# Moving the sampled keys, the softmax sums and the value rounds to earlier steps of a hybrid decoder layer

## The reference, cut to what matters

```
k_all = concatenate([ck[page_table], k]);  v_all = concatenate([cv[page_table], v])
s = einsum('bqhd,bkhd->bhqk', q, k_all) * dh ** -0.5 + c[past] - c[keys]
p = softmax(s, axis=-1)
out = einsum('bhqk,bkhd->bqhd', p, v_all)
```

## Time and profile before

| what | value |
|---|---|
| median of 3 runs | 1890.67 us (1890.24 to 1895.3) |
| the profiled execution's own time | 1893.1 us |
| its span, first to last instruction | 1891.4 us |
| PE busy, share of the span | 1803.2 us, 95% |
| DVE busy | 730.6 us, 39% |
| mean granted TensorE clock | 0.962 of full speed |
| pairs 0 to 3, from the first tile's scores of each | 102.33, 192.09, 282.94 and 372.26 us to 463.55 us |
| value rounds 0 to 15 | 450.68 to 553.74 us |

### The profile page before, as it was taken

The page is one execution under the profiler, slowest core; times in us unless marked ns, Lnnn a source line. Parts: engine busy times, 40 slices in busy tenths (PEclk is TensorE's granted clock), DMA queues, the critical chain, the costliest instruction groups (busy, mean ns, idle before and its releaser), DMA issues.

```text
span 1891.4 us, 29215 instructions
## 1 busy us (share of the span) xinstructions
PE 1803.2 (95%) x11360; PEld 1632.1 (86%) x11360; DVE 730.6 (39%) x1303; ACT 363.3 (19%) x691; POOL 502.5 (27%) x295
## 2 busy tenths in 40 slices
PE   5999999998999999999999989999999999999994
PEld 5966666665777879999999979999999999999993
DVE  3156766542415443121138754223213313312318
ACT  3132222322413223111120340100000010010022
POOL 3310101100210303332234524223232233322225
PEclk8999999998987979999999989999999999999997
DMA  5134434302642201111112212111111111111102
GB/s 155 54 108 122 118 116 117 122 25 80 180 143 47 56 8 50 44 44 54 46 34 72 63 34 59 54 44 44 44 44 53 36 55 44 44 46 54 45 23 90
DMA packets 173120, 126.39 MB, mean 67 GB/s; under 512 B 22266, under 2 KB 146570, under 8 KB 173042
## 3 DMA queue, kind: packets, MB, share of 16 engines
q1 hardware_dynamic: 169490, 124.09, 22.3%
q10 hardware_dynamic: 3552, 1.25, 0.3%
HBM read 115.45 MB, written 9.85 MB: 66 GB/s over the span
## 4 chain that ended last, share of the span: by engine, by line
PE 88%; DVE 5%; issue 2%; DMA 2%; ACT 2%; POOL 1%; SPq 1%; POOLq 0%; ACTq 0%; DVEq 0%
PE psum L741 14%; PE psum L745 14%; PE psum L744 14%; PE psum L819 4%; PE psum L825 4%; PE psum L823 4%; PE psum L1277 4%; PE psum L1276 4%; PE psum L1272 4%; PE psum L974 4%; PE psum L947 2%; PE psum L1225 2%; PE psum L1229 2%; PE psum L1228 2%; PE psum L950 1%
## 5 line engine op out<-in xcount | busy, mean ns | idle before, releaser
L689 POOL CAST wh<-raw 128x1024 fp32r<-128x1024 f32 x132 | 143.5, 1087 | 1342.9 <-PE psum L819 436.4
L741 PE MATMUL psum<-xh,wh 128*128 128x344 f32 (+1 forms) x1488 | 478.6, 322 | 6.5 <-POOL wl L691 3.6
L745 PE MATMUL psum<-xh,wl 128*128 128x344 f32 (+1 forms) x1488 | 476.4, 320 | 0.0
L744 PE MATMUL psum<-xl,wh 128*128 128x344 f32 (+1 forms) x1488 | 476.2, 320 | 0.0
L691 POOL TENSOR_TENSOR wl<-raw,wh 128x1024 fp32r<-128x1024 f32 x132 | 328.8, 2491 | 10.6
L741 PEld LDWEIGHTS psum<-xh,wh 128*128 128x128 f32 x1488 | 280.8, 189 | 7.6 <-issue 7.3
L744 PEld LDWEIGHTS psum<-xl,wh 128*128 128x128 f32 x1488 | 280.8, 189 | 0.2
L745 PEld LDWEIGHTS psum<-xh,wl 128*128 128x128 f32 x1488 | 280.7, 189 | 0.0
L2320 DVE TENSOR_TENSOR hf<-sg,psum 128x344 f32<-128x344 f32 x66 | 33.8, 513 | 385.0 <-PE psum L745 385.0
L819 PE MATMUL psum<-xh,wh 128*128 128x352 f32 (+1 forms) x480 | 164.0, 342 | 1.1 <-DVE negc_tok L1840 1.1
L823 PE MATMUL psum<-xl,wh 128*128 128x352 f32 (+1 forms) x480 | 161.2, 336 | 0.0
(11 more groups left out here) (305 smaller groups left out, 2621.8 us busy)
## 6 DMA issues: line engine op xcount, KB each, us to landing
raw<-in_w_in SPq DMA_DIRECT2D x86, 256.0 KB, 3.3
parts<-in_cache_k SPq DMA_DIRECT2D x64, 256.0 KB, 3.0
parts<-in_cache_v SPq DMA_DIRECT2D x64, 256.0 KB, 2.9
raw<-in_w_gate SPq DMA_DIRECT2D x44, 256.0 KB, 3.1
raw<-in_w_up SPq DMA_DIRECT2D x44, 256.0 KB, 3.2
raw<-in_w_down SPq DMA_DIRECT2D x44, 256.0 KB, 2.7
raw<-in_w_o SPq DMA_DIRECT2D x28, 256.0 KB, 3.0
cb<-negc_scratch SPq DMA_DIRECT2D x8, 520.0 KB, 5.3
```

The lines of the kernel that those rows point to most:

```text
L689: pool.tensor_copy(wh[:, s, :], raw[:, r, :]).then_inc(sem("panel_high"), 1)
L741: first = mm(out, w[0], x[0], start=(n == 0), stop=False)
L744: mm(out, w[0], x[1], start=False, stop=False)
L745: last = mm(out, w[1], x[0], start=False, stop=(n == len(ks) - 1))
```

## The change

Three lists of step numbers and one new list are edited, and the calls in the programs of PE, DVE, ACT and SP follow them. The keys' parts stood in 32 of the steps 3 to 51 (pairs 0, 1 and 2: 10, 12 and 10 parts); they now stand in every step from 3 to 34 (15 parts in pair 0, 17 in pair 1). The sums move closer together by one step and the exponentials from step 12 to 11. Value rounds 0 to 5 stand in steps 12 to 17 of pair 3, with the first two samples' outputs in steps 15 and 17; ten rounds are left for the front in place of twelve, each sample's outputs now ahead of the next sample's first round, and the last output ahead of the turned values. The panel loads in SP's program move with the rounds.

```diff
-KEYS_AT = [3 + 50 * c // PARTS for c in range(PARTS)]
-SUMS_AT = {8: (1, 2), 10: (3,), 11: (4,), 13: (5,)}
-ROUNDS_AT = {14: 0, 15: 1, 16: 2, 17: 3}
+KEYS_AT = [3 + c for c in range(PARTS)]
+SUMS_AT = {8: (1, 2), 9: (3,), 10: (4,), 12: (5,)}
+ROUNDS_AT = {12 + r: r for r in range(6)}
+OUTPUTS_AT = {15: 0, 17: 1}
...
-            for r in range(4, ROUNDS):
-                p = {4: 21, 6: 22, 9: 23, 12: 24}.get(r)
+            for r in range(6, ROUNDS):
+                p = {6: 21, 8: 22, 11: 23, 14: 24}.get(r)
...
+                    if x in OUTPUTS_AT:
+                        sample_outputs(OUTPUTS_AT[x])
                     if x in ROUNDS_AT:
                         value_round(ROUNDS_AT[x])
                 for _ in range(HALF_SLICE):
                     next(filler, None)
-            sample_outputs(0)
...
             whole(G0 - 1, 1, "gate")
-            value_round(4)
-            sample_outputs(1)
+            sample_outputs(2)
+            value_round(6)
             whole(G0 - 1, 2, "gate")
-            value_round(5)
+            value_round(7)
             whole(G0, 0, "q")
-            value_round(6)
-            sample_outputs(2)
+            sample_outputs(3)
+            value_round(8)
...
             whole(G0 + 2, 1, "v0")
-            value_round(13)
+            value_round(15)
             whole(G0 + 2, 2, "v0")
-            value_round(14)
-            sample_outputs(6)
...
             turn((ke,), FRONT["kt"], [])
-            value_round(15)
+            sample_outputs(7)
...
             whole(G0 + 3, 0, "v1")
-            sample_outputs(7)
...
-                if (j, x) == (3, 12):
+                if (j, x) == (3, 11):
                     act.wait_ge(sem("sdiff_ready"), 2)
...
-                    if x == 16:
-                        own(0)
-            own_out(0)
-            own(1)
+                    if x in (14, 16):
+                        own((x - 14) // 2)
+                    if x in (15, 17):
+                        own_out((x - 15) // 2)
+            own(2)
```

More of the change, by code:

```diff
@@ L1078, in _ @@
             whole(G0 - 1, 1, "gate")
-            value_round(4)
-            sample_outputs(1)
+            sample_outputs(2)
+            value_round(6)
             whole(G0 - 1, 2, "gate")
-            value_round(5)
+            value_round(7)
             whole(G0, 0, "q")
-            value_round(6)
-            sample_outputs(2)
+            sample_outputs(3)
+            value_round(8)
             whole(G0, 1, "q")
-            value_round(7)
+            value_round(9)
             whole(G0, 2, "q")
-            value_round(8)
-            sample_outputs(3)
+            sample_outputs(4)
+            value_round(10)
             whole(G0 + 1, 0, "k")
-            value_round(9)
+            value_round(11)
             whole(G0 + 1, 1, "k")
-            value_round(10)
-            sample_outputs(4)
+            sample_outputs(5)
+            value_round(12)
             whole(G0 + 1, 2, "k")
-            value_round(11)
+            value_round(13)
             whole(G0 + 2, 0, "v0")
-            value_round(12)
-            sample_outputs(5)
+            sample_outputs(6)
+            value_round(14)
             whole(G0 + 2, 1, "v0")
-            value_round(13)
+            value_round(15)
             whole(G0 + 2, 2, "v0")
-            value_round(14)
-            sample_outputs(6)
             for b in FRONT["k"]:
@@ L2079, in _ @@
             logits(0, FRONT["logits"])
-            own_out(1)
-            own(2)
+            own_out(2)
+            own(3)
             decay_rows(0)
             decayed_q(0, FRONT["q"][0])
-            own_out(2)
+            own_out(3)
             decayed_q(1, FRONT["q"][1])
-            own(3)
+            own(4)
             decayed_q(2, FRONT["q"][2])
-            own_out(3)
+            own_out(4)
             decayed_k(0, FRONT["k"][0])
-            own(4)
+            own(5)
             decayed_k(1, FRONT["k"][1])
-            own_out(4)
+            own_out(5)
             decayed_k(2, FRONT["k"][2])
-            own(5)
-            own_out(5)
             own(6)
```

## The result

The changed kernel takes 1896.6 us in the median (1888.9 to 1903.7, 20 runs); the kernel before took 1893.0 us (1888.1 to 1897.4, 20 runs) beside it. The ratio is 1.0021, 95% interval 1.0012 to 1.0031: slower, by 2 to 6 us. Twenty runs of each resolve less than the 0.3% that the prediction took for the limit. The profiled execution took 1895.1 us with a span of 1893.4, 2.0 us more than before.

The account below looks back on a forecast made before the run. PE's own work was taken to bound the pairs, the value rounds' transfers the pace after them. Waits +6.5 and clock +2.0 from denser keys, -5.2 from sums and rounds, made +3.3 us: 1894.0 us, range 1886 to 1904.

Parts of the forecast that it names:

- part 2: Moved sums and value rounds, pair 3 and the front: -5.2 us in all, between -3.1 and -6.9.
- step 11 of pair 1: PE waits 3.1 us for the k2 unit, behind DVE's query wait, key part and division.
- step 16 of pair 0: PE waits longer for DVE's last copy, behind a late query and the part of step 15: +2.1 us.
- step 5 of pair 1: Key parts of steps 3 and 4 hold up maxima, repeating pair 0's 0.94 us wait: +1.0 us.
- step 6 of pair 0: A small added wait of PE from the denser keys: some 0.3 us.
- clock, part 1: Clock falls after PE's waits in the pairs with denser keys: +2.0 us, two falls of 1.39 less one.
- part 1: Denser keys in pairs 0 and 1: +6.5 us of PE waits, with 2.0 us more for the clock.
- waits, part 2: From pair 3 on: output inside a wait -1.05, moved rounds +0.2, front -0.4, round 15 -1.9; together -3.1 us.
- clock, part 2: Half-speed instructions regain speed: an output -0.8, round 15 -0.9, the turn after it about -0.4 us.
- (A): SP becomes the bound in pairs 0 and 1, all seven query changes reach PE: +13, 1904 us; chance 0.30 with (C).
- (B): DVE's waits stay within PE's slack except step 5 of pair 1: gain 4 to 6 us, 1885 to 1887; chance 0.25.
- (C): Rounds keep their transfers' pace and gain only the 1.99 us: whole +6.5, 1897 us; chance 0.30 with (A).

Follow-up runs that it names:

- Experiment 6: Changed kernel with no key part in step 9 of pair 1, its eight later parts one step on; 1892.57 us, ratio 1.0011 to the kernel before.
- experiment 3: Changed kernel with two query buffers, each sample's query loaded one sample ahead; 1889.89 us, ratio 0.998 to the kernel before.
- experiment 9: Changed kernel with value rounds 14 and 15 each one chunk later; 1897.99 us, ratio 1.0029 to the kernel before.
- Experiment 10: Changed kernel with the last rounds, 14 and 15, exactly in the order of the kernel before; 1901.16 us, ratio 1.0041 to the kernel before.
- experiment 2: Changed kernel with the keys' parts back in their old steps, so only the rounds' change remains; 1886.9 us, ratio 0.9964 to the kernel before.
- experiment 4: Changed kernel with the 64 small forget-value loads moved on SP from pairs 0 and 1 to pair 2; 1892.7 us, ratio 0.9994 to the kernel before.
- experiment 7: Changed kernel with two query buffers and no key part in steps 4 and 9 of any pair; 1884.59 us, ratio 0.9964 to the kernel before.
- 8: Changed kernel with two query buffers and the keys' parts in their old steps; 1885.37 us, ratio 0.9965 to the kernel before.
- 1: Kernel before with only the keys' 32 parts moved to steps 3 to 34; 1902.87 us, ratio 1.0048 to the kernel before.
- 5: Changed kernel with only round 15 put back behind the turned keys, last output behind a chunk; 1894.3 us, ratio 1.0014 to the kernel before.

## Why the prediction came out as it did

The sign and the size of the whole were right: +3.3 us predicted, +2.0 in the profiled spans and +3.6 in the medians. The median itself lies 2.6 us above the 1894.0, nearly all of it because the kernel before also ran 2.3 us slower in these runs than in those that the prediction was set against. That part 2 came out near its -5.2 us is luck, as two errors in it cancel (below). Term by term, by the profiled executions:

| term | predicted | measured |
|---|---|---|
| step 11 of pair 1 | +3.1 | +3.51 |
| step 16 of pair 0 | +2.1 | +1.38 |
| step 5 of pair 1 | +1.0 | +0.95 |
| step 6 of pair 0 | +0.3 | nothing |
| step 11 of pair 0 | not seen | +0.93 |
| clock, part 1 | +2.0 | +1.92 |
| waits, part 2 | -3.1 | -1.48 |
| clock, part 2 | -2.1 | -4.40 |
| sum | +3.3 | +2.8 |

The rest of the kernel adds 0.1 us ahead of pair 0 and takes 0.9 off behind the start of the recurrent state, which makes the +2.0.

**Step 11 of pair 1: right, in mechanism and size.** The chain was the one predicted, query, part, division, unit; it only began later. Experiment 6 shows that the part in step 9 is what ties them, and experiment 3 that 2.5 of the 3.5 us go with the query's transfer; the 1.0 that it leaves is the part and the multiplication in GpSimd's split. The wait is 0.4 us above the forecast; the key product alone took 0.58 us more than the 1.22 that the prediction has. In the other executions the wait was 2.6 to 3.5 us, and the same meeting sets which: in the three with 3.51 us GpSimd's cast began 0.1 to 0.3 us ahead of the product, which then took 1.80, 1.95 and 2.03 us; in the two with 2.61 and 2.62 the product began no later than the cast, took 1.23, and the cast took twice its 1.04. The two in experiment 9:

```profile
248.37 1.23 DVE L1922 TENSOR_TENSOR parts<-parts,qb 128x1024 f32<-128x1024 f32 x1 [3.53 <-DMA qb<-sq_scratch]
...
248.38 2.11 POOL L690 CAST wh<-raw 128x1024 fp32r<-128x1024 f32 x1 [23.93 <-PE psum L820]
```

**Step 16 and step 11 of pair 0: one term too large, since one was missed.** The walk forecast the query's issue at 182.8 (182.79), the part at 186.7 (186.84) and the freed bank at 190.9 (191.08). But it measured the wait from PE's old time, 188.55 (a difference of 2.35 us, of which it charged 2.1 without saying why); PE had already lost 0.93 us in step 11 and came later. I had stopped the walk at "ends at 163.0 in the old kernel and by my walk in the new one" without asking what the later division meets: the multiplication ran into GpSimd's split. The two together are 2.31 us, near the 2.1. A delay upstream eats the slack that a later wait is charged for, so waits in one chain don't simply add.

**Six waits for the query, not seven**, 15.3 us in the range of 15 to 20: one landed in time. Its transfer landed 3.1 to 4.0 us after the issue (3.6 in the median), so the row that was taken held. The estimate of 2.6 us by the Trainium skill's page "DMA: Bandwidth & Descriptors", section on the anatomy of one DMA, whose fit is for GpSimd's queue, did not hold on SP's queue here. What the prediction works out from that estimate doesn't follow from its own terms either: two waits shorter by 1.3 us leave 6.5 - 2.6 = 3.9 us for part 1 and 5.9 with the clock, not 3, and so a loss of 0.7 us for the whole and not a gain of 2.

```profile
DMA to landing us min/median/max: 3.1/3.6/4.0
```

**Part 2: the gain was right, its kind wrong.** The step that failed is the sum of the waits, -3.1, and in it "Round 15 now follows a chunk and no longer waits 1.99 us behind a short turn: about -1.9", with "the turn after round 15 about -0.4" for the clock. Round 15 still waits 0.75 us (0.75 to 1.42 in the seven kernels that have it there), so this term was -1.24. The 0.83 us of `o_copied` is new; the prediction did not ask what the output of sample 0 had covered where it stood. The turns wait another 0.33 us. The other terms held: -1.40 for the second of the last two waits (-1.05 forecast; the two together are the 5 us that the prediction names as its sign), -0.39 for the front (-0.4). In all the waits gave 1.48 us, not 3.1.

The clock gave twice what I took. From the turn of the keys to the recurrent state PE's busy time fell from 19.73 to 16.36 us, 1.0 of it round 15 itself, which moved ahead, so 2.3 us of clock against my 1.3, and the granted clock rose from 0.86 to 1.00. I had counted the instructions that ran at half speed in the one row behind the wait; the low level went on past them. Experiment 10 undoes this place alone and loses 0.83 us of idle time and 3.08 of clock. The other 2.1 us came ahead of the turn, against my 0.8, and repeat badly: the output of sample 0 runs in 1.05 us as forecast, but that of sample 1, which now stands between the last two waits, took 1.87 in eight of the ten kernels with the changed rounds.

Over all seven executions with the round order of the change (2, 3, 4, 6, 7, 8 and the changed kernel) against the two with the old one (the kernel before and 1), the stretch has 2.2 us less idle time and 3.4 less busy time in the mean. So both errors, of the waits and of the clock, are there in the mean too; with two executions on one side and values that spread by 1 to 2 us, their sizes are not known better than to about a microsecond.

**The rivals.** (A) needs SP late by a microsecond on average; it was 1.4 to 1.6 us late at three of the seven queries and on time at four, 0.7 in the mean, and experiment 4 took its lateness away and kept most of the waits, though it gave back about half of the time that the dense keys cost above the rounds alone (0.27 of 0.57%). (B) fell with the waits in steps 11 and 16. (C) fell with experiment 2: the rounds alone are worth 6.8 us.

**The clock term of part 1 was right by luck.** Its 2.0 us came out as 1.92, but the same instructions in pairs 0 to 2 kept PE busy for 264.25, 265.88, 267.38, 271.32 and 272.42 us in five executions. The idle time, 9.4 to 11.2 us, repeats much better.

## What to carry to other kernels

When a single buffer is refilled only after its last use, ask what stands behind the next use in the same engine's program: the engine that needs those instructions pays for the transfer, and an empty step ahead of them or a second buffer takes the price away. Before a piece of work is moved, ask which wait it covered where it stood. Put at least one long piece of other work between two pieces that wait for each other's transfer; the clock that falls with the wait can cost more than the wait. Split a difference into the bound engine's idle time and its busy time before naming a cause, and time the halves of an edit alone: here one gained 6.8 us and the other lost 9.1, and the kernel with the first alone beats both.

## What the runs showed of the hardware that was not expected

The same wait may or may not bring the clock down. In step 16 of pair 0 the clock stayed up after waits of 1.66, 1.67 and 1.95 us (experiments 10, 9 and 6; the step grew by its wait alone) and fell after 1.34, 1.66, 2.11 and 2.55 us (experiments 4, 1 and 5 and the changed kernel). After the waits of 1.16 or 1.17 us in step 16 it fell in four places of all the traces (pair 1 of the kernel before and of experiments 3 and 8, pair 2 of experiment 7). A fall cost 1.6 us in one execution and 5.3 in another, with the same instructions behind it. In step 11 of pair 1 the clock fell after each of the three waits of 3.51 us, after the 2.48 of experiment 4, and after one of two of 2.6. Where DVE's key product and GpSimd's cast met in step 10 of pair 1, the one that began later was held (the product 1.80 to 2.03 us in place of 1.22, or the cast 2.11 in place of 1.04): the order of two starts, 0.1 to 0.3 us apart, set a wait of PE at 2.6 or 3.5 us.
